# Second norm of the first block, done per tile of 128 tokens

## The reference

```
def _modulate(x, g, shift, scale):
    return _rmsnorm(x, g) * (1 + scale) + shift

def first_block(...):
    for l in range(DEPTH):
        ...
        mix_x, _ = _token_mix(h, lp, ang, kv_c)      # ends with (g_a*y_a + g_b*y_b + g_c*y_c) @ w_out
        x = x + m_x[2] * mix_x
        h2 = _modulate(x, norm2_g[l], m_x[3], m_x[4])
        x = x + m_x[5] * _peer(h2, w_pq[l], peer_keys[l], peer_down[l], peer_up[l])
        if not last:
            ...                                        # the same for ctx
    return _rmsnorm(x, final_g)

def _peer(h, w_pq, peer_keys, peer_down, peer_up):
    q = (h @ w_pq).reshape(B, L, PEER_HEADS, 2, PEER_QDIM // 2)
    s = jnp.einsum("blhpd,hpkd->blhpk", q, peer_keys)
    sv, si = lax.top_k(s, PEER_TOPK)
    ...   # the 16 best of 256 sums per head, a softmax over them: 128 experts per token
    # a = peer_down[experts] . h ; out = (gates * gelu(a)) @ peer_up[experts]
```

## Time and profile before

| | |
|---|---|
| median of 3 runs | 4059.99 us (4055.05 to 4064.07) |
| the profiled execution | 4068.35 us, span 4066.5 us |
| PE busy | 3459.0 us, 85% |
| DVE busy | 2335.6 us, 57% |
| POOL busy | 1515.2 us, 37% |
| ACT busy | 952.1 us, 23% |
| moved by DMA | 1156.80 MB, mean 284 GB/s |

### The profile page before, as it was taken

How to read it: one execution, slowest core, us unless ns; L and a number is a source line. 1 busy time by engine, 2 the same in 40 slices (tenths; PEclk the granted TensorE clock), 3 DMA queues, 4 the chain that set the end, 5 groups by cost and what they waited for, 6 DMA issues and landing times. The chain is left out here.

```text
span 4066.5 us, 43125 instructions
## 1 busy us (share of the span) xinstructions
PE 3459.0 (85%) x14118; PEld 2188.7 (54%) x14118; DVE 2335.6 (57%) x5070; ACT 952.1 (23%) x1946; POOL 1515.2 (37%) x1757
## 2 busy tenths in 40 slices
PE   6999986988896887888878877777789979999999
PEld 2476653454463343344445422222279869798898
DVE  2313789354557777545433776666555776565565
ACT  1301211121112111221131111111123543334433
POOL 0000566555556666666510567677710000000000
PEclk7999998999998898989989999999999979999999
DMA  6566999998899999999923899999955415454444
GB/s 268 193 259 223 379 381 357 365 343 320 343 361 346 362 392 372 359 371 382 367 105 115 340 371 383 382 381 390 391 192 189 153 47 186 179 186 174 149 169 155
DMA packets 274031, 1156.80 MB, mean 284 GB/s; under 512 B 30913, under 2 KB 31681, under 8 KB 235458
## 3 DMA queue, kind: packets, MB, share of 16 engines
q0 software_dynamic: 221184, 805.40, 52.1%
q1 hardware_dynamic: 52674, 349.23, 23.2%
HBM read 1153.47 MB, written 1.05 MB: 284 GB/s over the span
## 5 line engine op out<-in xcount | busy, mean ns | idle before, releaser
L1038 PE MATMUL ps<-rows,diag 128*128 128x512 f32 x2048 | 965.1, 629 | 233.0 <-DMA rows<-in_peer_up,iup 218.6
L2065 DVE CUSTOM_DVE_ANT_0 rows<-rows,ps 128x1024 f32<-128x1024 f32 x512 | 613.1, 1219 | 433.3 <-DMA rows<-in_peer_down,idown 410.4
L1038 PEld LDWEIGHTS ps<-rows,diag 128*128 128x128 f32 x2048 | 403.2, 201 | 772.8 <-issue 461.2
L998 PE MATMUL ps<-rows,diag 128*128 128x512 f32 x1024 | 511.9, 625 | 183.9 <-DMA rows<-in_peer_up,iup 175.8
L2620 POOL DMA_INDIRECT rows<-in_peer_down,idown x512 | 489.2, 955 | 411.8 <-PE ps L1038 310.0
L2620 POOL DMA_INDIRECT rows<-in_peer_up,iup x512 | 485.9, 949 | 239.6 <-DVE a L2065 125.0
L1090 PE MATMUL ps<-hT_hi,w_hi 128*128 128x256 f32 x1600 | 453.6, 284 | 8.9 <-DVE hT_lo L2194 8.9
L998 PEld LDWEIGHTS ps<-rows,diag 128*128 128x128 f32 x1024 | 176.2, 191 | 518.1 <-DMA rows<-in_peer_up,iup 387.7
L1092 PE MATMUL ps<-hT_lo,w_hi 128*128 128x256 f32 x1600 | 453.6, 284 | 0.0
L1091 PE MATMUL ps<-hT_hi,w_lo 128*128 128x256 f32 x1600 | 452.6, 283 | 0.0
L2009 DVE CUSTOM_DVE_ANT_0 rows<-rows,ps 128x1024 f32<-128x1024 f32 x256 | 308.2, 1220 | 212.5 <-DMA rows<-in_peer_down,idown 210.1
(11 more groups left out here) (322 smaller groups left out, 4309.9 us busy)
## 6 DMA issues: line engine op xcount, KB each, us to landing
wring<-in_wgu SPq DMA_DIRECT2D x66, 1024.0 KB, 4.7
wring<-in_wdn SPq DMA_DIRECT2D x33, 1024.0 KB, 4.8
wring<-in_wG SPq DMA_DIRECT2D x29, 1024.0 KB, 8.4
rows<-in_wmod SPq DMA_DIRECT2D x27, 1024.0 KB, 8.0
wring<-in_wpq SPq DMA_DIRECT2D x24, 1024.0 KB, 7.1
rows<-in_wgu SPq DMA_DIRECT2D x22, 1024.0 KB, 4.8
wring<-in_wmod SPq DMA_DIRECT2D x21, 1024.0 KB, 7.0
rows<-in_peer_down,idown POOLq DMA_INDIRECT x768, 6.4
```

Source lines behind the costliest of these rows:

```text
L998: ins = pe.matmul(ps[:, UPB + half, :], diag[:, j % DIAGS, :], rows[:, s, half * 512:(half + 1) * 512], start=(first and j == 0), stop=(la ...
L1038: ins = pe.matmul(ps[:, UPB + half, :], diag[:, j % DIAGS, :], rows[:, j, half * 512:(half + 1) * 512], start=(first and j == 0), stop=(la ...
L2065: dve.tensor_tensor_reduce(out=rows[:, j, :], in0=rows[:, j, :], in1=h_ps, scale=1.0, scalar=0.0, op0=ALU.mult, op1=ALU.add, accum_out=a8[ ...
```

## The change

For x0 and x1 (`by_tile_from`) the stretch goes tile by tile. In all three runs the last two output chunks are held: both stay in their slots, PE does tile 0 with both, then tile 1 with both. For x0 and x1 the four broadcast rows stand between the two tiles, and the stage `norm` does nothing more on PE. `hT` transposes tile 0 only. The first two query chunks are waited for together, both are used for tile 0, then tile 1 is transposed, then both are used for tile 1; each such matmul has 128 columns, not 256. DVE makes the gain first, then root, h and shift of tile 0, then the output sum, root, h and shift of tile 1; its scratch for the output sum moves to `junk`. ACT takes the squares of each tile as soon as its x is there; in its program both stand ahead of the copies of `hT`. c0 uses the same DVE code (sum of tile 1 at the start of `norm`), but keeps its order on PE. SP's program is unchanged.

```diff
+        def by_tile_from(run, k):
+
+            return k == 1 and run != "c0"
...
             def norm(run, k):
+                if not by_tile_from(run, k):
+                    norm_rows(run, k)
+
+            def norm_rows(run, k):
                 for half in range(2):
                     bcast(("bs", run, k, half), run, 1 + 3 * k, half)
                 for half in range(2):
@@ -710,20 +718,27 @@
             hT_now = [None]
 
             def hT_(run, k):
+                hT_now[0] = (run, k)
+                if by_tile_from(run, k):
+                    for a in range(2):
+                        turned(run, k, 0, a)
+                    return
+                for a in range(2):
+                    for t in range(TT):
+                        turned(run, k, t, a)
...
@@ -944,11 +959,37 @@
                 at_mark(pe, "mixT", run, 4)
                 if c == 0:
                     bcast(("bm", run, half), run, 2, half)
-                token_major([("o", run, half, t) for t in range(TT)], mixT, 512, c)
+                keys = [("o", run, half, t) for t in range(TT)]
+                if half == 0:
+                    token_major(keys, mixT, 512, c)
+                    return
+
+                def part(c, t):
+                    for k in range(4):
+                        last = pe.matmul(ps[:, job_bank[keys[t]], :], mixT[:, 4 * c + k, t * P:(t + 1) * P], out_w[c][:, k * 512:(k + 1) * 512],
+                                         start=(c + k == 0), stop=(c == 1 and k == 3))
+                    if c == 1:
+                        ended(last, keys[t])
+                    elif t == 0:
+                        ended(last, keys[0] + ("part",))
+
+                if c == 0:
+                    for key in keys:
+                        job(key)
+                out_w[c] = chunk()
+                part(c, 0)
+                if c == 1:
+                    if by_tile_from(run, 1):
+                        norm_rows(run, 1)
+                    part(0, 1)
+                    part(1, 1)
+                    chunk_end(2)
+
+            out_w = {}
...
+                def first_queries():
+                    ws = [chunk() for _ in range(2)]
+                    bs = [job(("qp", run, n)) for n in range(2)]
+                    for t in range(TT):
+                        for a in range(2):
+                            if t:
+                                turned(run, 1, t, a)
+                        for a in range(2):
+                            at_evac(pe, ("hT", run, 1, t, a))
+                        for n in range(2):
+                            for hp in range(2):
+                                for k in range(KT):
+                                    last = pe.matmul(bs[n][:, hp * TOK + t * P:hp * TOK + (t + 1) * P], ws[n][:, k * 256 + hp * P:k * 256 + (hp + 1) * P],
+                                                     hT[:, k, t * P:(t + 1) * P], start=(k == 0), stop=(k == KT - 1))
+                            if t:
+                                ended(last, ("qp", run, n))
+                                chunk_end()
+
+                if c < 8 and not by_tile_from(run, 1):
+                    queries(c)
+                elif c == 0:
+                    first_queries()
+                elif 2 <= c < 8:
                     queries(c)
...
@@ -1358,21 +1421,25 @@
             def norm(run, k):
                 s = RUNS[run][0]
                 if k:
-                    at_mark(act, "resid", run, 4)
+                    pass
                 elif RUNS[run][1] == 0:
                     act.wait_ge((ld_x, ld_c)[s], 16)
                 else:
                     at_mark(act, "fin", ("x0", "c0")[s], 2)
                 for t in range(TT):
+                    if k:
+                        at_mark(act, "resid", run, 3 + t)
                     squares(x[s][:, t, :], t, h[s][:, t, :]).then_inc(mark["ss"], 1)
...
             def hT_(run, k):
+                    for t in range(1 if by_tile_from(run, k) else TT):
+                        turned(run, k, t, a)
...
+                if c == 0 and by_tile_from(run, 1):
+                    for a in range(2):
+                        turned(run, 1, 1, a)
...
-                for half in range(2):
-                    at_evac(act, ("bh", run, 1, half))
+                if t or not by_tile_from(run, 1):
+                    for half in range(2):
+                        at_evac(act, ("bh", run, 1, half))
...
+            def norm_by_tile(run):
+                s = RUNS[run][0]
+                if not by_tile_from(run, 1):
+                    mixed(run, 1, 1)
+                gains[0] += 1
+                dve.wait_ge(ld_gain, 16 * gains[0])
+                for half in range(2):
+                    cols = slice(half * 512, (half + 1) * 512)
+                    key = ("bs", run, 1, half)
+                    b = at_mm(dve, key)
+                    release(dve.scalar_tensor_tensor(amul[:, cols], b, 1.0, gain[:, cols], ALU.add, ALU.mult), key)
+                for half in range(2):
+                    at_evac(dve, ("bs", run, 1, half))
+                for t in range(TT):
+                    if t and by_tile_from(run, 1):
+                        mixed(run, 1, t)
+                    dve.wait_ge(mark["ss"], norm_mark(run, 1, t + 1))
+                    rsqrt(ss[:, 6 + t:7 + t], ss[:, t:t + 1], 1, D)
+                    ins = dve.scalar_tensor_tensor(h[s][:, t, :], x[s][:, t, :], ss[:, 6 + t:7 + t], amul[:, :], ALU.mult, ALU.mult)
+                    if t:
+                        ins.then_inc(gain_used, 1)
+                        dve.wait_ge(gain_used, gains[0])
+                    else:
+                        v(ins)
+                    for half in range(2):
+                        cols = slice(half * 512, (half + 1) * 512)
+                        key = ("bh", run, 1, half)
+                        ins = dve.tensor_tensor(h[s][:, t, cols], h[s][:, t, cols], at_mm(dve, key), ALU.add)
+                        if t:
+                            release(ins, key)
+                        else:
+                            ins.then_inc(mark["h"], 1)
+
             def norm(run, k):
+                if k:
+                    norm_by_tile(run)
+                    return
...
             def out_(run, half, c):
                 if c == 0:
                     return
+                at_evac(dve, ("bm", run, half))
+                for t in range(TT - half):
+                    mixed(run, half, t)
+
+            def mixed(run, half, t):
+
                 s = RUNS[run][0]
                 cols = slice(half * 512, (half + 1) * 512)
-                at_evac(dve, ("bm", run, half))
-                for t in range(TT):
-                    key = ("o", run, half, t)
-                    b = at_mm(dve, key)
-                    release(dve.tensor_tensor(amul[:, t * 512:(t + 1) * 512], b, mb[:, cols], ALU.mult), key)
-                    at_evac(dve, key)
-                    dve.tensor_tensor(x[s][:, t, cols], x[s][:, t, cols], amul[:, t * 512:(t + 1) * 512], ALU.add).then_inc(mark["resid"], 1)
+                key = ("o", run, half, t)
+                b = at_mm(dve, key)
+                tmp = junk[:, t * 512:(t + 1) * 512]
+                release(dve.tensor_tensor(tmp, b, mb[:, cols], ALU.mult), key)
+                at_evac(dve, key)
+                dve.tensor_tensor(x[s][:, t, cols], x[s][:, t, cols], tmp, ALU.add).then_inc(mark["resid"], 1)
```

More of the change, by code:

```diff
@@ L712, in hT_, with turned @@
             def hT_(run, k):
-                s = RUNS[run][0]
                 hT_now[0] = (run, k)
+                if by_tile_from(run, k):
+                    for a in range(2):
+                        turned(run, k, 0, a)
+                    return
                 for a in range(2):
                     for t in range(TT):
-                        if k == 2:
-                            pass
-                        elif t == 0:
-                            pe.wait_ge(mark["h"], norm_mark(run, k, a + 1))
-                        else:
-                            at_evac(pe, ("bh", run, k, a))
-                        b = job(("hT", run, k, t, a))
-                        for j in range(4):
-                            last = pe.transpose(b[:, j * P:(j + 1) * P], h[s][:, t, (4 * a + j) * P:(4 * a + j + 1) * P], ident[:, :])
-                        ended(last, ("hT", run, k, t, a))
+                        turned(run, k, t, a)
+            def turned(run, k, t, a):
+                s = RUNS[run][0]
+                if k == 2:
+                    pass
+                elif t == 0:
+                    pe.wait_ge(mark["h"], norm_mark(run, k, a + 1))
+                else:
+                    at_evac(pe, ("bh", run, k, a))
+                b = job(("hT", run, k, t, a))
+                for j in range(4):
+                    last = pe.transpose(b[:, j * P:(j + 1) * P], h[s][:, t, (4 * a + j) * P:(4 * a + j + 1) * P], ident[:, :])
```

(25 more changed lines are left out.)

1 line of the change is left out of this document (removed).

## The result

The changed kernel takes 4080.19 us (median of 7 runs, 4072.64 to 4085.44) against 4059.99 (7 runs, 4049.12 to 4067.56): ratio 1.0049, 95% interval 1.0035 to 1.0063. Timed again beside other runs it gave 1.0036 [1.0021, 1.0051]. Both together, weighted by their intervals, are 1.0043, some 17.4 us [13.3, 21.6]. The forecast was 4066.8 with a range up to 4075.0: the direction was right and the size too small, and the first median lies outside the range. The profiled execution took 4080.19 us (span 4078.1), 11.8 more than that of before; 3.5 of them lie ahead of x0's stretch, where no instruction was changed.

A forecast was written before the change was run, and what follows sets the result against it. The prediction took the chain of waits from the gathers back through PE's first two query chunks as the bound. Terms of 3.5 (x1), 3.0 (x0) and 0.3 (c0) made 6.8 us over 4059.99: 4066.8 us, range 4056 to 4075.

The forecast's parts named there:

- the first pass: At x1, tile 0's queries with both chunks take 7.1 us plus 1.8 us lost at half pace.
- the gap: Between the query passes, 8 transposes (1.0) and ScalarE's last copy (1.0): 2.0 us without queries on PE.
- mechanism: At x0, the second query chunk is issued right behind keysT and queries begin when it lands; first score 3.0 us later.
- the clock's term: First queries after PE's idle time run 3.6 us at half pace, losing 1.8 us; bounds 0 and 3.5.
- the weights don't decide: Rival, chance 0.06: second query chunk is there when tile 0's copies are; x1 8.0, x0 5.8 us early, 4046.2 us.
- the clock stays low: Rival, chance 0.20: low clock lasts twice as long and returns in the second pass; 3.5 us more per place, 4073.8 us.
- Absorption in full: Rival, chance 0.14: the first gather groups make good a start 3 us later; about 4061 us.
- the sum of 6.8: Total slowdown in us: x1 3.5, x0 3.0 and c0 0.3 later.
- The c0 term: At c0, DVE's extra rsqrt of 2.4 us is nearly all taken up by existing waits; 0.3 us, bounds 0 and 2.4.
- c0 unchanged: Expected sign in the changed profile: c0 looks as it did before; no size given.
- A microsecond there should be a microsecond at the end: At PE's first two query chunks, on the chain of waits to the gathers, each microsecond counts once at the end.

The follow-up runs named there:

- one_chunk_c0_old: Changed kernel with only the first query chunk by tile at x0 and x1, and c0's part undone; ratio 0.9978 to the kernel before.
- c0_sum_early: Changed kernel with c0's second output sum done in its output stage, ahead of the 8 row products; ratio 1.0049 to the kernel before.
- wpq_first: Changed kernel with SP issuing the second query chunk of x0 and x1 ahead of keysT; ratio 1.0011 to the kernel before.
- one_chunk: Changed kernel with only the first query chunk by tile, the second multiplied afterwards for all 256 tokens; ratio 0.9993 to the kernel before.
- c0_old: Changed kernel with all of c0's part undone, x0 and x1 still by tile; ratios 1.0035 and 1.0026 to the kernel before.
- x0_only: Kernel before with x0 alone by tile, both first query chunks together; ratios 1.0023 and 0.9999 to the kernel before.
- x0_one_chunk: Kernel before with x0 alone by tile, and only its first query chunk by tile; ratio 0.9993 to the kernel before.
- x1_only: Kernel before with x1 alone by tile, x0 and c0 as before; ratio 1.0004 to the kernel before.
- x1_one_chunk: Kernel before with x1 alone by tile, and only its first query chunk by tile; ratio 0.9984 to the kernel before.
- c0_only: Kernel before with c0's part of the change alone, x0 and x1 as before; ratio 0.9996 to the kernel before.
- pe_pad: Kernel before with 128 further waits on PE at its start, for constants already landed; ratio 1.0000 to the kernel before.
- x0_delay: Kernel before with PE multiplying x0's first query chunk three times over instead of once; ratio 1.0046 to the kernel before.
- x1_delay: Kernel before with PE multiplying x1's first query chunk three times over instead of once; ratio 1.0031 to the kernel before.

## Why the prediction was right and where it was wrong

**x1, right to a tenth.** From the half's first output matmul: keysT at 21.6 (predicted 21.7), the first query at 28.9 (29.0), the first pass 8.9 (8.9, 1.8 of it for the clock), the gap 1.9 (2.0), the first score at 46.9 (47.0); 3.5 us late. Its cause is shown: asking for the second chunk later takes the wait away.

**x0, mechanism right, the clock's term mis-sized.** The first query at 29.1 (29.15), but the first pass takes 10.0, not 8.9: PE is at it for 5.7 us at the low clock (3.6 at x1), which costs 2.7 against the second pass of 7.2, not 1.8. The view of 378 to 380 us (columns as in the earlier trace rows, with all engines) has the end of it, a mean granted clock of 0.77:

```profile
378.00:380.00 2.00, 2.00 (x16) 2.00 (x15) 0.00 (x0) 0.00 (x0) 0.00 (x0) 0.77 0.00 0
```

x0 is 4.0 us late instead of 3.0.

**The rivals.** That the weights don't decide is refuted by the wait for the DMA. That the clock stays low is refuted in its second half: the second pass takes 7.2 us at both places, and the granted clock is 1.00 through the transposes between the passes. Absorption in full is refuted by the two delays.

For the rule of the Trainium skill ("TensorE: Matmul & The Clock Gate", Part 4) that transposes don't count, the gap between the passes is no test, since a longer one left the clock high too: in one_chunk_c0_old PE does nothing but transposes from 2196.11 to 2200.02, and the granted clock stays at 1.00. What speaks against the rule is the kernel before, as the prediction read it: nothing but transposes ran from 2208.22 until the queries at 2212.93, and the clock had risen by then (before, 2212 to 2213 us: granted clock 0.96):

```profile
2212.00:2213.00 1.00, 0.07 (x1) 0.96 1.02 434
```

**The step that failed is the sum of 6.8** (3.5 + 3.0 + 0.3), where 17.4 [13.3, 21.6] was measured. Its terms for the two places were nearly right: 3.5 and 4.0 in the profile, 7.5 to 8.6 together. Two other parts of it were not.

*The c0 term* (0.3) was worked out from DVE's extra root alone; the moved matmuls and the wait for the bank were missed, though PE's banks and the place of `mixed(run, 1, 1)` stand in the code. "c0 unchanged" was the one sign in the prediction's list that the profile went against. Alone this costs nothing measurable, beside x0 and x1 likely some 5 us.

*"A microsecond there should be a microsecond at the end"* held for plain delays, but I also took it that what lies behind a place is moved and not changed. With c0 as before, the places give 7.2 to 8.9 against 12.9 [8.8, 17.0]. Taking each kernel's places away from its measured change, as a comparison made afterwards over the whole table, leaves:

| changed stages | kernels | left over its places, us |
|---|---|---|
| x0, c0 and x1 | changed (2), c0_sum_early (c0 in part), wpq_first, one_chunk | 9.1 +- 2.3 |
| x0 and x1 | c0_old (2), one_chunk_c0_old | 3.4 +- 3.2 |
| x0 | x0_only (2), x0_one_chunk | 3.6 +- 3.5 |
| x1 | x1_only, x1_one_chunk | -1.4 +- 3.8 |
| c0 | c0_only | -1.6 +- 4.9 |
| none | pe_pad, x0_delay, x1_delay | 0.5 +- 2.8 |

The places are from one profile each and kernels of one series share their runs of the kernel before, so the uncertainties are somewhat larger than given. By this table some 3 to 4 of the missing 9 us come with x0 by tile, and 5.6 [1.7, 9.5] with c0's part beside the others.

Of the first part the profiles show one spot. Behind c0's last gather come the keys and values of c1 and then x1, with no gather beside them, and their first large product is, after:

```profile
2087.53 13.84 PE L754 MATMUL ps<-wring,hT 128*128 128x416 f32 x32 [0.95 <-issue]
```

and before:

```profile
2083.60 11.41 PE L739 MATMUL ps<-wring,hT 128*128 128x416 f32 x32 [0.94 <-issue]
```

These are the same 32 records, 2.4 us longer, since the clock is granted at 0.50 for 20.5 us instead of 13.7 around them, while PE's idle time in front of the transposes there is about the same (10.1 and 10.5 us). Eight of the eleven profiles with x0 by tile have the long form (13.5 to 13.8 us), none of the seven without. From PE's last sum of c0's gathers to x1's stretch, where no instruction was changed, the eleven take 119.6 us on average (115.8 to 121.4) and the seven 117.1 (115.8 to 119.0). So about 2.5 us of the missing 9 seem to lie here, more than the spread between the profiles would give by chance. Why x0 by tile and this go together isn't settled: x0_delay, whose x0 is later still, has the short form.

The granted clock as a whole fits, and shows no more. Its mean over 85 executions of the kernel before on the three faster chips is 0.9490. From the two levels that is (1 - 0.9490) x 2 x 4059 = 414 us at 1.2 GHz; the changed kernel has 433 and 425. Its places account for 6.8 of these (10.2 instead of 6.8 us in the stretch at x0, 13.7 instead of 10.2 at x1), and the spot above for 6.8 more. But x0_delay, with nothing by tile, has 427 too. The rest of the missing time, most of it c0's share, has no place in the profiles (on the faster chips, the time from x0's first score to x1's stretch is 1797.6 us on average in the five profiles with x0 by tile and c0's part, and 1798.0 in the three with x0 by tile and without it) and stays open.

## What to carry to other kernels

When work is split to start earlier, list what its first instruction waits for and follow each of these to its own queue: a load behind an event of the later part makes the split worthless, and asking for it one step later turned 3.5 us of loss at x1 into 7 of gain. Follow shared code into the stage that "isn't changed", on every engine and through its buffers in turn. And leave room in the range for what several small shifts do together: parts that measured 7.5, 1.6 and -1.6 us alone were 17 together, 10 more with an uncertainty of 9.

## What was not expected of the hardware

Kernels timed on another chip took some 98 us longer, the kernel before too (4158.95 us against 4059.82 to 4061.70). There the gathers are slower and hardly anything else. No profile of the kernel before was taken there, but in x1_one_chunk x1's gathers, from POOL's first start at 2273.6 to PE's last sum at 3061.7, take 788.1 us against 736.5 before, and everything behind them 1090.5 against 1090.2. PE's stretches were as on the others (36.06 against 36.04 us at x1). Ratios to the kernel before on the same chip can be compared, absolute times can't.
